# Experts taken in order of use, users of the least used one first in their group's slots, and five expert steps on 64 columns

## The reference, cut to what matters

```python
g_prob = softmax(ht @ w_rg + b_rg);  g_val, g_idx = top_k(g_prob, 1)       # 1 of 4 groups
e_in   = (ht @ w_re + b_re)[group g_idx]                                   # its 4 experts
e_val, e_idx = top_k(softmax(e_in), 2);  e_val = e_val / sum(e_val)        # 2 of these 4
combine = one_hot(4 * g_idx + e_idx) * (g_val * e_val)
a = einsum('td,edf->tef', ht, w_gate);  u = einsum('td,edf->tef', ht, w_up)    # 16 experts
hid = silu(a) * u * combine
out = einsum('tef,efd->td', hid, w_down)                                   # D_EXPERT = 256
```

## Time and profile before

| | us |
|---|---|
| median of 3 runs (771.08 to 772.08) | 771.19 |
| span of the profiled execution | 770.4 |
| PE busy | 762.7 (99%) |
| DVE busy / ACT busy | 556.1 (72%) / 469.0 (61%) |
| expert weights asked for by SP, first to last | 563.4 to 720.5 |
| first and last matmul of the expert steps | 569.8 to 738.5 |

### The profile page before, as it was taken

One profiled execution on the slowest core, in us unless ns is written; L12 is line 12 of the kernel. 1 busy time (PEld: TensorE's weight loads), 2 busy tenths in 40 slices (PEclk: granted clock), 3 DMA queues, 4 the chain that ended last, 5 costly groups with the idle time before them and its releaser, 6 DMA issues.

```text
span 770.4 us, 12090 instructions
## 1 busy us (share of the span) xinstructions
PE 762.7 (99%) x4808; PEld 645.0 (84%) x4808; DVE 556.1 (72%) x672; ACT 469.0 (61%) x580; POOL 33.6 (4%) x62
## 2 busy tenths in 40 slices
PE   8999999999999999999999999999999999999998
PEld 8989878888998978888888998888787787878877
DVE  7898895575779797667577777458688594848865
ACT  7785596535587668644568645444575463737655
POOL 5500000000000000300000000000000000000000
PEclk9999999999999999999999999999999999999999
DMA  8666244555446435466645345654068796969921
GB/s 284 198 226 203 80 162 151 192 184 185 137 149 212 162 116 186 137 218 165 211 146 183 117 157 170 212 176 152 1 246 300 256 373 231 358 250 374 351 99 55
DMA packets 70040, 149.60 MB, mean 194 GB/s; under 512 B 8458, under 2 KB 11104, under 8 KB 69984
## 3 DMA queue, kind: packets, MB, share of 16 engines
q1 hardware_dynamic: 69568, 148.78, 56.3%
q0 software_dynamic: 384, 0.04, 0.2%
q10 hardware_dynamic: 32, 0.01, 0.0%
HBM read 147.76 MB, written 1.05 MB: 193 GB/s over the span
## 4 chain that ended last, share of the span: by engine, by line
PE 95%; DVE 1%; DMA 1%; ACT 1%; issue 0%; SPq 0%; POOL 0%; DVEq 0%; POOLq 0%; ACTq 0%
PE mm L646 19%; PE mm L648 18%; PE mm L647 18%; PE mm L662 4%; PE mm L663 4%; PE mm L664 4%; PE aux L1188 4%; PE aux L1190 4%; PE aux L1189 4%; PE aux L757 3%; PE aux L646 1%; PE aux L648 1%; PE aux L647 1%; DMA sb_raw<-in_w_up 1%; PE aux L797 1%; PE aux L1174 1%
## 5 line engine op out<-in xcount | busy, mean ns | idle before, releaser
L1831 DVE TENSOR_TENSOR sb_w_lo<-sb_raw,sb_w_hi 128x2048 fp32r<-128x2048 f32 (+2 forms) x148 | 306.7, 2081 | 85.0 <-ACT sb_w_hi L1314 41.5
L1314 ACT ACTIVATE sb_w_hi<-sb_raw 128x2048 fp32r<-128x2048 f32 (+1 forms) x83 | 155.4, 1872 | 117.6 <-PE mm L648 88.3
L646 PE MATMUL mm<-sb_w_hi,sb_hT_hi 128*128 128x512 f32 (+1 forms) x456 | 176.0, 386 | 0.0
L647 PE MATMUL mm<-sb_w_lo,sb_hT_hi 128*128 128x512 f32 (+1 forms) x456 | 172.8, 379 | 0.0
L648 PE MATMUL mm<-sb_w_hi,sb_hT_lo 128*128 128x512 f32 (+1 forms) x456 | 172.8, 379 | 0.0
L1656 ACT ACTIVATE sb_w_hi<-sb_raw 128x2048 fp32r<-128x2048 f32 x44 | 84.3, 1918 | 41.3 <-DMA sb_raw<-in_w_up 26.4
L646 PEld LDWEIGHTS mm<-sb_w_hi,sb_hT_hi 128*128 128x128 f32 x456 | 85.9, 188 | 17.3 <-issue 2.0
L648 PEld LDWEIGHTS mm<-sb_w_hi,sb_hT_lo 128*128 128x128 f32 x456 | 85.9, 188 | 16.2
L647 PEld LDWEIGHTS mm<-sb_w_lo,sb_hT_hi 128*128 128x128 f32 x456 | 86.0, 189 | 14.9
L662 PE MATMUL mm<-sb_hT_hi,sb_w_hi 128*128 128x256 f32 x272 | 78.4, 288 | 0.0
L663 PE MATMUL mm<-sb_hT_lo,sb_w_hi 128*128 128x256 f32 x272 | 77.0, 283 | 0.0
(11 more groups left out here) (429 smaller groups left out, 1136.6 us busy)
## 6 DMA issues: line engine op xcount, KB each, us to landing
sb_raw<-in_w_in SPq DMA_DIRECT2D x120, 512.0 KB, 4.6
sb_raw<-in_w_down SPq DMA_DIRECT2D x32, 512.0 KB, 5.7
sb_raw<-in_w_gate SPq DMA_DIRECT2D x31, 512.0 KB, 5.2
sb_raw<-in_w_up SPq DMA_DIRECT2D x31, 512.0 KB, 6.9
sb_raw<-in_w_out SPq DMA_DIRECT2D x16, 512.0 KB, 4.3
sb_raw<-in_w_up_attn SPq DMA_DIRECT2D x8, 512.0 KB, 4.4
sb_raw<-in_w_up_hgrn SPq DMA_DIRECT2D x8, 512.0 KB, 4.3
sb_raw<-in_w_o SPq DMA_DIRECT2D x8, 512.0 KB, 4.2
```

Source lines behind the costliest of these rows:

```text
L646: pe.matmul(dst, a_hi, rhs[0], start=start, stop=False, skip_group_check=True)
L647: pe.matmul(dst, a_hi, rhs[1], start=False, stop=False, skip_group_check=True)
L1314: act.activation(w_hi[:, slot(t), 0:width], raw[:, slot(t), 0:width], ACT.Copy).then_inc(hi_split, 1)
L1831: return dve.tensor_tensor(out_, a, b, op)
```

## The change

The step table is written out by hand. `ORDER` gives (place of the group, expert of the group) for the sixteen steps. `windows(s)`: the largest group is on both windows for three of its experts and on window 0 alone for the fourth, the second group is on window 1, the third on window 0, the fourth on window 1. `half(s)`: the five steps on 64 columns are all four of the fourth group (last 64 slots) and one of the third (first 64 slots). To make that valid, the slots are laid out third group, largest, second, fourth; in each group the expert with the fewest users is found, the tokens that use it come first in the group's slots, and the experts are numbered from it on in a circle, so that expert 3 in `ORDER` is the least used one. Steps 2, 4, 8, 9 and 13 are on 64 columns now.

Around it: the top-2 choice is made before the group order, with comparisons on 2 x 4 x 4 values in place of 10 x 4 x 4; two more matmul pairs count the users (`uses`) and rank those of the least used expert (`used_ranks`); `order_ready` is counted twice, once for the four experts of the largest group and once for the other twelve; the exponentials and their wait move behind the first gather on ACT; the three dummy matmuls are gone; the routing weights are multiplied out after a rotation; POOL makes a second set of unsplit 64 columns.

```diff
-WHOLE_TILES = [AT_TILE["up%d" % part, s] for s in range(3, STEPS - 1, 4) for part in range(2)]
-WINDOWS = [(0, 1), (0,), (1,), (1,)]
+ORDER = [(0, 0), (1, 0), (3, 0), (2, 0), (3, 1), (1, 1),
+         (0, 1), (2, 1), (3, 2), (2, 3), (0, 3),
+         (0, 2), (2, 2), (3, 3), (1, 2), (1, 3)]
+def windows(s):
+    j, k = ORDER[s]
+    return ((0, 1) if k < 3 else (0,), (1,), (0,), (1,))[j]
+def half(s):
+    return {(3, 0): 1, (3, 1): 1, (3, 2): 1, (3, 3): 1, (2, 3): 0}.get(ORDER[s])
+BANKS = [None, 2, 0, 2, 0, 2, None, 2, 0, 1, 2, None, 2, 0, 2, 0]
...
 def whole(s):
-    return s % 4 == 3 and s < STEPS - 1
+    return half(s) is not None
...
                 if kind == "up0":
+                    if s == 1:
+                        sp.wait_ge(S["order_ready"], 2)
+                    expert.append(sp.value_load(order_i[0:1, column(s):column(s) + 1], min_val=0, max_val=EXPERTS - 1))
...
+            def uses():
+                pe.wait_ge(S["use_ready"], 1)
+                for tt in range(TT):
+                    last = pe.matmul(aux[1][:, W:W + 16], ones[:], taken_of[:, tt].rearrange("p g e -> p (g e)"),
+                                     start=tt == 0, stop=tt == 1)
+                last.then_inc(S["use_counted"], 1)
...
             ple(1, 0, 0)
             ranks()
+            uses()
             ple(1, 0, 1)
             ple(1, 1, 0)
+            used_ranks()
             ple(1, 1, 1).then_inc(tile_done, 1)
-            keep_busy(3)
...
-                for w in WINDOWS[s % 4]:
+                for w in windows(s):
...
             gathered_high(0)
+            act.wait_ge(S["shift_ready"], 1)
+            act.activation(exps_[:, :], shifted[:, :], ACT.Exp).then_inc(S["exp_ready"], 1)
```

## The result

The changed kernel takes 778.26 us (median of 4 runs, 775.22 to 778.69), the kernel before 771.63 beside it (771.08 to 772.18). The ratio is 1.0072, 95% interval 1.0057 to 1.0087: slower by 0.7%, where 771.1 was forecast and 774.5 was the upper end of the range. The profiled executions have spans of 776.7 and 770.4, 6.3 apart. Every time in this document is of fast runs; the only slow one, an execution of e1 at 1068.56 us with a granted clock of 0.65, is left out.

What follows compares the result with a forecast made beforehand. PE, 99% busy, was taken as the bound, with loads close behind. PE work -11.0, head +2.6 and waits +8.3 gave -0.1: span 770.3, plus 0.8 for the median, 771.1 us; range 766.5 to 774.5.

Steps and rivals of the forecast that it cites:

- PE's work: Expert steps: fewer full `up` and `down` windows, more 64-column parts, -11.0 us in all.
- The head: Everything up to the first expert matmul, plus routing weights and short matmuls behind it: +2.6 us, bounds +1.9 to +3.5.
- The holes ahead of the gather: PE idle about 0.4, 0.8 and 1.5 us where the dummies stood, inside the head's delay.
- The waits for loads: Expert steps: PE waits for late tiles behind 64-column steps, +8.3 us, bounds 1.5 to 11.7.
- The mechanism: Expert loads: a tile behind a 64-column tile is asked for only when PE has used that one.
- four waits: At `up1` of step 5, `down` 7, `up1` of step 10 and step 15's transposes: 2.4, 1.6, 0.5, 3.8 us.
- the list: The places in the expert steps where PE would wait; other tiles cost nothing or were covered by the next wait.
- the sum: Whole kernel: -11.0 + 2.6 + 8.3 = -0.1 us, given a chance of 0.43.
- the last burst: Loads behind step 13: seventh tile 23.4 us after issue, making PE wait 3.8 at step 15's transposes.
- Loads that land sooner: Rival for the bursts: first tile after 4.7 us, bursts 2 us shorter, 766.6 us in all; chance 0.32.
- slow `down` tiles: Rival: `down` tiles take 1.0 us more each in the last burst, +3.3 us in all, 774.4 us; chance 0.20.
- The clock: Rival for the gather: PE's clock falls to 1.2 GHz behind idle holes, about 774 us; chance 0.05.

Runs made afterwards that it cites:

- e1: The changed kernel with dummy matmuls in the three holes of PE ahead of the gather: 776.74 us, ratio 1.0068.
- e12: e11 with e1's dummy matmuls and the expert numbers of steps 2 to 15 read early on SP: 768.55 us, ratio 0.9956.
- e7: The changed kernel with its sixteen steps reordered, 64-column steps at 3, 6, 7, 8 and 10, last three full: 772.39 us, ratio 1.0004.
- e6: The changed kernel's head with the step table of the kernel before: 775.97 us, ratio 1.0049.
- e9: The changed kernel with step 9 on a full window, POOL's second set of 64 columns left out: 777.15 us, ratio 1.0067.
- e10: The changed kernel with steps 9 and 13 on full windows, POOL's second set left out: 772.45 us, ratio 1.0005.
- e2: e1 plus 12 dummy matmuls ahead of the transposes of step 15: 777.23 us, ratio 1.0066.
- e8: e7 with e1's dummy matmuls and expert numbers 2 to 15 read early on SP: 772.39 us, ratio 1.0005.
- e11: The changed kernel with only two 64-column steps, 3 and 12, in a new order, POOL's second set left out: 769.24 us, ratio 0.9971.
- e3: The changed kernel with step 15's silu and `hidden` ahead of the splits of its `down` tile: 777.45 us, ratio 1.0083.
- e5: The kernel before with each expert tile from the third on loaded at half its columns: 771.13 us, ratio 0.9985.

## Why the prediction was wrong, point by point

*PE's work.* Right. The sum above closes with the -11.0 to within half a microsecond. e12, with a full clock and three short waits, shows it more directly: PE is busy for 160.3 us up to the scatter, 7.3 less than before, where two 64-column steps in place of five leave a forecast of -7.0, or -6.7 with the short matmuls.

*The head.* Right where the clock holds: the order at 564.63 + 0.17 (forecast 564.6), the picks at 567.44 (567.3), the gather at 568.11 (568.0), the first expert matmul at 572.06 in e7 (572.05). The holes ahead of the gather are there too, 0.38, 0.70 and 1.33 (0.4, 0.8 and 1.5). What was missing is what comes of it behind: the measured price of the head by e6 is 4.0 us, not 2.6. Its profile has two falls of the clock, the profile of before has none: at the transposes behind the slots it is 4.8 us late, and over the rest of the steps it wins 0.9 of it back, in part at each 64-column step, for which no row names the cause.

*The waits for loads.* This is the step that failed, together with the clock below. The mechanism was right and four waits stand where they were put, smaller than forecast: 1.47 (2.4), 0.91 (1.6), under 0.25 before the second half of step 10 (0.5), 3.40 (3.8). But the list had an end, "Steps 2 and 4's other tiles and step 13's first ... no wait", and waits of over 0.4 came at six places that it didn't have: `down`s 0, 2 and 3 (0.56, 0.41, 0.58), the first half of step 6 (0.47), that of step 11 (1.19), the transposes of step 14 (0.57). In all PE is idle for 10.2 us more than before, 9.8 without the slots' longer wait, where 8.3 were in the sum; with what each wait costs at its two ends, between 11 and 12 us, some 3 more than forecast. That is about half of the 6.4 by which the profile's span was missed. The forecast followed each 64-column step to the one tile behind it that was worst, as if the ring were full again at the next. It isn't: a 64-column step takes about 6.8 us of PE for its three tiles (3.76 for `up`, 2.73 for `down` and 0.36), while the tiles of the last burst, once it ran, came 3.3 apart (the six behind the first, from 712.89 to 732.57), so 9.8 for three. A one-window step has 8.2 and gains nothing back either; only a two-window step does. That a step's place in the order matters this way is what e7 shows, and e9 and e10 show the size of it: the saving of a fourth and a fifth such step is nothing or less than nothing.

*Loads that land sooner,* the rival with 0.32: the first of a burst did come sooner, 5.6 after its issue for the wait at 625.05 and 4.7 in the last burst in place of 6.1. (The Trainium skill, DMA: Bandwidth & Descriptors, section on the anatomy of one DMA, gives by its fit an estimate of 4.4 for 1 MB. That section is on DMAs of GpSimd, one for all the bytes; here SP issues two of 512 KB, and the last burst comes near to the figure, the others do not.) But the seventh came after 24.4, not 23.4. What the first tile won, two of the four `down` tiles lost: they came 4.4 and 4.0 us behind the tile ahead, the other two 3.0 and 2.5, and the two `up` tiles 3.3 and 2.6. That is half the mechanism of the *slow `down` tiles*, to which 0.20 was given, with its 774.4: ACT waits 17.5 us for `w_down` in the expert steps, 10.2 before. Neither rival alone, and both in the same burst. Why these two were slow no run shows.

*The clock,* put at nothing in the sum and at 0.05 as a rival, for one place. That was the other term of the sum that failed: the profile of the change has two falls, which take up to 3.1 us of it (1.5 and 1.6 above), against a profile of before without one. It is not an accident of this one execution. The mean granted clock was 0.995 to 0.997 in all four runs of the change, and 0.997 to 1.000 in the 58 runs of the kernel before beside the experiments. As a share of the spans this is an estimate of 3.1 and 0.6 us on average, so at most 2.5 us of the 6.6, and less where PE would have waited anyway: e7 has 3.5 us of it and is level with the kernel before. e1 removed the fall in the head, and e2 both, but e2's profile has another one, and neither was faster beyond its interval. So the share of the clock stays open between nothing and 2.5. The Trainium skill, TensorE: Matmul & The Clock Gate, section on what is actually happening, says that an idle PE runs at half clock. The rows agree in part: 0.50 in 569 to 571, behind the hole of 1.33, but in only two of eight profiles with such a hole; and behind the wait of 3.40 the first four matmuls of the `down` still go at full clock.

*The reads of expert numbers on SP,* one ahead of each step, were not costed. In the burst 1.6 us lie between the issue of a `down` at 710.29 and the next at 711.87, where the kernel before has 1.0 (606.07 to 607.08). e8 and e12, which move them and add the dummies at once, show no measurable worth of both together.

The sign of the sum hung on terms of 11.0 and 8.3 that were not independent: the work is taken from PE by the very steps that drain the ring.

## What to carry to other kernels

When an engine is at 99% and the loads behind it run close, work taken away is worth only the lead that the ring has at that place: count the time that each group of steps gives the loads, over several groups in a row, before the time it saves. Short steps did best here when they were few and stood among long ones (e11), and beyond the number that these carry a longer step was no slower (e9) or faster (e10). What part of it comes from the later release of their buffers, by PE's end and not by the split, no run tried by itself. Where loads bind, a wait that is removed at one reader can come back at the next (e3). And to see whether they bind, make the same edit in the kernel before too: half the bytes gave 10.5 us in one kernel and 0.8 in the other.

## What the runs showed of the hardware

The granted clock of PE fell behind waits of 0.7 to 3.4 us, for 3 to 6 us each, and not at a fixed place. The length of the wait alone does not decide: among the longer ones those of 1.98 (e3), 1.99 (e7), 2.55 (e1), 2.75 (e8), 3.30 (e9) and 3.40 (the change) were followed by a fall, those of 1.86 (e8), 2.09 and 2.46 (both e3) were not. Behind the last wait of the change it cost 1.6 us. A hole of 1.31 to 1.34 ahead of the gather stood in eight profiles and was followed by a fall in two of them; the wait for the slots, 0.7 to 1.1 us long and over by 583 to 588, stands in all fourteen profiles and was followed by one in six, among them e5, where it is 0.7 as in the kernel before, whose own profile shows none. In e7 it fell at the first wait in the middle:

```profile
650.50 0.50 PE L711 MATMUL mm<-sb_w_hi,sb_bT_hi 128*128 128x512 f32 x1 [1.99 <-DVE sb_w_lo L1912]
...
651.56 0.63 PE L711 MATMUL mm<-sb_w_hi,sb_bT_hi 128*128 128x512 f32 x1
```

A matmul row of 512 columns reads 0.39 at 2.4 GHz and 0.63 at 1.2 GHz (the starts are 0.23 and 0.43 apart). So a difference of 1.5 us between two single profiles of such kernels can be a fall of the clock that happened in one and not in the other. In the mean over the span it is only a step from 1.000 to 0.998, so compare that mean over all the runs of both kernels.
